# Two blocks of branch gates placed in the softmax pause, and the output projection done tile by tile with four weight buffers

## The reference

```python
def reference(x, positions, w_in, ...):
    proj = einsum('bsd,de->bse', x, w_in)
    aq, ak, av, hq, hf, hi, hg, ga, gh = split(proj)
    attn = sliding_window_gqa_sinks(aq, ak, av, attn_sinks, positions)   # chunks of 64, softmax with a sink
    rec = hgrn2(hq, hf, hi, hg, lb, hgrn_norm_g)                         # chunked recurrence, RMS norm, gate
    mixed = sigmoid(ga) * (attn @ w_proj_attn) + sigmoid(gh) * (rec @ w_proj_hgrn)
    x = layer_norm(ALPHA * x + mixed @ w_out, ln1_g, ln1_b)
    # peer_ffn: 8 heads, top 16 of 128 twice, top 16 of the sums, e = expert numbers, g = softmax of the scores
    hid = einsum('thkd,td->thk', u[e], x); act = gelu(hid)
    ffn = einsum('thk,thkd->td', g * act, v[e])
    return layer_norm(ALPHA * x + ffn, ln2_g, ln2_b)
```

## Time and profile before

| | |
|---|---|
| median of three executions | 1649.82 us (1645.25 to 1654.13) |
| the profiled execution: its own time | 1645.0 us |
| its span in the trace | 1643.2 us |
| PE busy | 1543.6 us, 94% |
| DVE busy | 1131.2 us, 69% |
| DMA over the span | 532.38 MB, 324 GB/s |
| granted PE clock, mean | 0.964 |

### The profile page before, as it was taken

The page is one execution under the profiler, slowest core; times in us unless marked ns, Lnnn a source line. Parts: engine busy times, 40 slices in busy tenths (PEclk is TensorE's granted clock), DMA queues, the critical chain, the costliest instruction groups (busy, mean ns, idle before and its releaser), DMA issues.

```text
span 1643.2 us, 17974 instructions
## 1 busy us (share of the span) xinstructions
PE 1543.6 (94%) x6542; PEld 1098.7 (67%) x6542; DVE 1131.2 (69%) x2364; ACT 270.4 (16%) x543; POOL 610.0 (37%) x518
## 2 busy tenths in 40 slices
PE   8798999789998799999999999889999999999997
PEld 7697778665557566888888888756666544444443
DVE  1413899978769999999979999366556735545523
ACT  2601213621010111111134453100000000000000
POOL 0000543466667463322322223465534633424100
PEclk9898998779999799999999999989999999999999
DMA  7586967777999797998978878999999999999962
GB/s 297 203 275 212 397 228 265 251 246 273 412 398 374 275 403 282 316 330 288 327 255 312 319 277 299 410 383 405 404 408 406 405 402 380 395 393 392 369 218 77
DMA packets 145511, 532.38 MB, mean 324 GB/s; under 512 B 14864, under 2 KB 34064, under 8 KB 133904
## 3 DMA queue, kind: packets, MB, share of 16 engines
q0 software_dynamic: 74016, 269.52, 43.7%
q1 hardware_dynamic: 70256, 244.94, 40.0%
q10 hardware_dynamic: 1152, 16.78, 2.6%
HBM read 503.92 MB, written 27.26 MB: 323 GB/s over the span
## 4 chain that ended last, share of the span: by engine, by line
PE 74%; DVE 12%; DMA 7%; issue 3%; ACT 2%; POOL 0%; SPq 0%; DVEq 0%
PE bank L835 26%; PE bank L860 22%; PE bank L740 7%; PE bank L815 6%; PE bank L853 3%; DMA arena<-v_cols_d 3%; DVE arena L1163 2%; DMA arena<-gates_d 2%; DVE arena L1178 2%; PE bank L775 2%; PE bank L750 2%; PE bank L752 2%; PE bank L587 1%; PE bank L575 1%; DMA arena<-u_cols_d 1%
## 5 line engine op out<-in xcount | busy, mean ns | idle before, releaser
L1592 POOL DMA_INDIRECT arena<-u_d,arena x256 | 319.7, 1249 | 566.4 <-DVE arena L1163 315.9
L860 PE MATMUL bank<-arena 128*128 128x512 f32 x1024 | 448.2, 595 | 16.8 <-DVE arena L1501 14.1
L835 PE MATMUL bank<-arena 128*128 128x256 f32 x2048 | 452.9, 379 | 4.0 <-DMA arena<-u_cols_d 4.0
L835 PEld LDWEIGHTS bank<-arena 128*128 128x128 f32 x2048 | 386.6, 190 | 69.4 <-issue 17.8
L1592 POOL DMA_INDIRECT arena<-v_d,arena x256 | 288.9, 1129 | 362.9 <-DVE arena L1178 287.2
L860 PEld LDWEIGHTS bank<-arena 128*128 128x128 f32 x1024 | 195.1, 191 | 250.7 <-issue 227.2
L1178 DVE SCALAR_TENSOR_TENSOR arena<-arena 128x1024 f32<-128x1024 f32 x256 | 327.9, 1281 | 42.4 <-DMA arena<-v_d,arena 32.2
L1163 DVE CUSTOM_DVE_ANT_0 arena<-arena 128x1024 f32<-128x1024 f32 x256 | 304.2, 1221 | 68.5 <-DMA arena<-u_d,arena 67.9
L1501 DVE TENSOR_TENSOR arena<-arena 128x256 f32<-128x256 f32 x128 | 52.9, 420 | 159.5 <-DMA arena<-act_d 103.1
L1054 ACT ACTIVATE arena<-bank 128x256 f32<-128x256 f32 x128 | 49.2, 384 | 491.2 <-PE bank L835 491.1
L815 PE MATMUL bank<-arena 128*128 128x128 f32 (+1 forms) x512 | 118.9, 394 | 1.4 <-ACT arena L1021 1.4
(11 more groups left out here) (200 smaller groups left out, 1035.6 us busy)
## 6 DMA issues: line engine op xcount, KB each, us to landing
arena<-w_items_d SPq DMA_DIRECT2D x66, 1024.0 KB, 7.2
arena<-u_cols_d SPq DMA_DIRECT2D x128, 512.0 KB, 6.6
arena<-v_cols_d SPq DMA_DIRECT2D x128, 512.0 KB, 8.9
gates_d<-arena ACTq DMA_DIRECT2D x8, 2048.0 KB, 8.2
arena<-gates_d SPq DMA_DIRECT2D x16, 1024.0 KB, 16.7
act_d<-arena SPq DMA_DIRECT2D x8, 1024.0 KB, 9.3
arena<-act_d SPq DMA_DIRECT2D x8, 1024.0 KB, 16.7
arena<-u_d,arena POOLq DMA_INDIRECT x256, 8.7
```

The source lines that it names most:

```text
L835: last = mm(bank[:, 4 + c % 2, 0:ND], u_buf[:, c % UBUFS, k, :], B.act_in[:, k, B.n - ND:B.n], start=k == 0, stop=k == KC - 1)
L860: last = mm(bank[:, 2 * n + half, :], act_slot(i)[:, n * P:(n + 1) * P], v_buf[i % VBUFS][:, half * 512:(half + 1) * 512], start=i == 0, s ...
L1592: pool.indirect_dma_start(rows[:, r % SLOTS, :], None, table, bass.IndirectOffsetOnAxis(eidx[:, t, k:k + 1], 0)).then_inc(landed[r % SLOTS ...
```

## The change

It does five things. (1) `gates(0)` goes ahead of the first `turn_weights`, `gates(1)` behind the first two, in both fronts. They use PSUM banks 0 to 3, wait for all copies of the projections (`proj_out`), and ACT's sigmoids of them (`gate_sigmoids`) stand ahead of the recurrence's output copies; `chunk_kv(0)` waits for these. ACT's last projection copies move ahead of its scaling of the softmax. `turn_rec` now stands directly behind the last `tile_out`. (2) The output projection goes tile by tile, and the first two units sum six of their eight blocks ahead of the wait for the last two. (3) `RING` is 4, and two more items are loaded ahead of x and the input of front B. (4) DVE's rows: none at 161 and 170 within the output projection; `EARLY_ROWS` 196, `PAIR_ROWS` 8, `HOT_ROWS` 18. (5) `SPREAD_END` is 79: the 64 spreads lie in 27 hidden blocks, not in 30.

```diff
--- before.py
+++ after.py
@@ -45,7 +45,7 @@
 RMS_EPS = 1e-6
 
 
-RING, ITEMW = 3, 2048
+RING, ITEMW = 4, 2048
 TW = 256
 N_HQF, N_TOK, N_MIX, N_OUT, N_WQ = 4, TOKW // TW, 3 * KC // 2, D // TW, PH
 TOK_EARLY = 5
@@ -77,18 +77,18 @@
 EXP1_AT = 24
 EXP_AT = 49
 TURN_AT = 51
-SPREAD_AT, SPREAD_END = 52, 82
+SPREAD_AT, SPREAD_END = 52, 79
 ROOT0_Q = 44
 GELU1_AT = FIRST + 12
 PAIR = 2
-EARLY_ROWS, PAIR_ROWS, HALF_ROWS = 204, 7, 8
-HOT_ROWS = 30
+EARLY_ROWS, PAIR_ROWS, HALF_ROWS = 196, 8, 8
+HOT_ROWS = 18
 MID_ROWS = 314
 ACT_BACK_LEAD = 12
 
 
 AT_CUM, AT_SOFT, AT_HGRN, AT_SOFT2, AT_CAUSAL, AT_STATE, AT_REC, AT_MIX, PAIR_STEP = 44, 50, 52, 56, 64, 68, 76, 90, 16
-ODD_STEP, AT_OUT, OUT_STEP, HGRN_STEP, STATE_STEP = 5, 152, 9, 3, 2
+ODD_STEP, AT_OUT, HGRN_STEP, STATE_STEP = 5, 152, 3, 2
 ROUTE_ROWS = 6
 FG_HEAD, ROPE_HEAD = 4, 6
 ROUTE_STEPS = 17
...
@@ -379,8 +379,11 @@
 
         def out_units(F):
 
-            return ([(k, t) for k in range(N_OUT - 2) for t in range(F.nt)]
-                    + [(k, t) for t in range(F.nt) for k in range(N_OUT - 2, N_OUT)])
+            return [(k, t) for t in range(F.nt) for k in range(N_OUT)]
+
+        def gate_bank(m):
+
+            return 2 * m if m < 2 else 4 * (m % 2)
 
         def item(F, k):
 
@@ -463,13 +466,13 @@
                 sp.dma_start(dst, src).then_inc(consts_in, 16)
             for hh in range(2):
                 sp.dma_start(sinkc[CH * hh:CH * hh + CH, :], sinks[hh, :].partition_broadcast(CH)).then_inc(consts_in, 16)
-            for k in range(2, I_MIX):
+            for k in range(2, I_MIX + 2):
                 load(A, k)
             load_x(A)
             load_xT(B)
             for k in range(2):
                 sp.dma_start(ln_gb[:, k, :], ln1[k, :].partition_broadcast(P)).then_inc(ln_in, 16)
-            for k in range(I_MIX, ITEMS):
+            for k in range(I_MIX + 2, ITEMS):
                 load(A, k)
             for k in range(KEPT, ITEMS):
                 load(B, k)
@@ -659,10 +662,28 @@
                                     last = mm(o, before, p, start=False, stop=True)
                     last.then_inc(F.av_done, 1)
 
+                def gates(m):
+                    k = I_MIX + 3 * (m // 2) + m % 2
+                    item_in(pe, F, k)
+                    w = item(F, k).rearrange("p (c n) -> p c n", n=P)
+                    if m >= 2:
+                        pe.wait_ge(F.mix_out, m - 1)
+                    else:
+                        pe.wait_ge(F.proj_out, 2 * N_HQF + N_TOK * nt)
+                    b = gate_bank(m)
+                    for g in range(2):
+                        for c in range(KC):
+                            last = mm(bank[:, b + g, 0:n], w[:, g * KC + c, :], F.act_in[:, c, :],
+                                      start=c == 0, stop=c == KC - 1)
+                    last.then_inc(F.gate_done, 1)
+
+                gates(0)
                 pe.wait_ge(F.reached, V_ZERO)
                 turn_weights(0)
+                turn_weights(1)
+                gates(1)
                 for c in range(F.nc):
-                    if c + 1 < F.nc:
+                    if 0 < c < F.nc - 1:
                         turn_weights(c + 1)
                     times_v(c)
 
@@ -720,26 +741,13 @@
                         last = turn(bank[:, 6 + t % 2, h * P:(h + 1) * P], F.otok[:, t, h, :], ident[:, :])
                     last.then_inc(F.rec_turned, 1)
 
-                pe.wait_ge(F.proj_out, 2 * N_HQF + N_TOK * nt)
+                pe.wait_ge(F.gate_ready, 4)
                 chunk_kv(0)
                 for t in range(nt):
                     chunk_kv(2 * t + 1)
                     tile_out(t)
                     chunk_kv(2 * t + 2)
 
...
                 def branches(m):
                     k = I_MIX + 3 * (m // 2) + 2
@@ -755,9 +763,10 @@
 
                 pe.wait_ge(F.state_ready, states + 1)
                 for m in range(0, KC, 2):
-                    gates(m)
-                    gates(m + 1)
-                    if m == 0:
+                    if m:
+                        gates(m)
+                        gates(m + 1)
+                    else:
                         for t in range(nt):
                             turn_rec(t)
                         pe.wait_ge(F.rec_out, nt)
@@ -765,15 +774,25 @@
                     branches(m + 1)
 
 
+                def sum_out(u, c):
+                    k, t = out_units(F)[u]
+                    w = item(F, I_OUT + k).rearrange("p (c n) -> p c n", c=KC)
+                    return mm(bank[:, u % 4, 0:TW], F.mixT[:, c, t * P:(t + 1) * P], w[:, c, :],
+                              start=c == 0, stop=c == KC - 1)
+
+                pe.wait_ge(F.gate_ready, 2 * KC - 2)
+                pe.wait_ge(F.mix_out, KC - 2)
+                for u in range(2):
+                    item_in(pe, F, I_OUT + u)
+                    for c in range(KC - 2):
+                        sum_out(u, c)
                 pe.wait_ge(F.mix_out, KC)
                 for u, (k, t) in enumerate(out_units(F)):
                     item_in(pe, F, I_OUT + k)
-                    w = item(F, I_OUT + k).rearrange("p (c n) -> p c n", c=KC)
                     if u >= 4:
                         pe.wait_ge(F.y_out, u - 3)
-                    for c in range(KC):
-                        last = mm(bank[:, u % 4, 0:TW], F.mixT[:, c, t * P:(t + 1) * P], w[:, c, :],
-                                  start=c == 0, stop=c == KC - 1)
+                    for c in range(KC - 2 if u < 2 else 0, KC):
+                        last = sum_out(u, c)
                     last.then_inc(F.y_done, 1)
 
 
@@ -970,13 +989,13 @@
                 copy_tok(TOK_EARLY)
                 decays(2)
                 decays(3)
+                for k in range(TOK_EARLY + 1, N_TOK):
+                    copy_tok(k)
                 for c in range(F.nc):
                     act.wait_ge(F.soft_den, c // (F.nc // 2) + 1)
                     for j in range(PAIRS):
                         last = fn(F.SC[:, c, j, :], F.SC[:, c, j, :], ACT.Copy, scale=F.den[:, c, j:j + 1])
                     last.then_inc(F.soft_done, 1)
-                for k in range(TOK_EARLY + 1, N_TOK):
-                    copy_tok(k)
 
                 def copy_wT(c):
                     act.wait_ge(F.w_turned, c + 1)
@@ -995,6 +1014,15 @@
                     fn(F.kendT[:, t, :, :], bank[:, 4 + t % 2, :].rearrange("p (h k) -> p h k", h=HH),
                        ACT.Copy).then_inc(F.kend_out, 1)
 
+                def gate_sigmoids(m):
+                    act.wait_ge(F.gate_done, m + 1)
+                    if m >= 2:
+                        act.wait_ge(F.mix_out, m - 1)
+                    for k in range(2):
+                        fn(F.sig[:, m % 2, k, :], bank[:, gate_bank(m) + k, 0:n], ACT.Sigmoid).then_inc(F.gate_ready, 1)
+
+                gate_sigmoids(0)
+                gate_sigmoids(1)
                 for t in range(nt):
                     act.wait_ge(F.o_done, t + 1)
                     fn(F.otok[:, t, :, :], bank[:, 2 + t % 2, :].rearrange("p (h e) -> p h e", h=HH), ACT.Copy).then_inc(F.o_out, 1)
@@ -1007,11 +1035,8 @@
                             act.wait_ge(F.rec_turned, t + 1)
                             fn(F.recT[:, :, t * P:(t + 1) * P], bank[:, 6 + t % 2, :].rearrange("p (h k) -> p h k", h=HH),
                                ACT.Copy).then_inc(F.rec_out, 1)
-                    act.wait_ge(F.gate_done, m + 1)
                     if m >= 2:
-                        act.wait_ge(F.mix_out, m - 1)
-                    for k in range(2):
-                        fn(F.sig[:, m % 2, k, :], bank[:, 4 * (m % 2) + k, 0:n], ACT.Sigmoid).then_inc(F.gate_ready, 1)
+                        gate_sigmoids(m)
                     if F is B and m == GELU_M:
                         act.wait_ge(hid_ready, 1)
                         fn(hid, hid, ACT.Gelu).then_inc(gelu_done, 1)
@@ -1336,8 +1361,8 @@
                 dve.wait_ge(F.x_in, 16)
                 dve.wait_ge(ln_in, 32)
                 for u, (k, t) in enumerate(out_units(F)):
-                    if t == 0 and k < N_OUT - 1:
-                        rows_until(AT_OUT + OUT_STEP * k)
+                    if u == 0:
+                        rows_until(AT_OUT)
                     dve.wait_ge(F.y_done, u + 1)
                     xs = F.x1[:, t, k * TW:(k + 1) * TW]
                     v.scalar_tensor_tensor(out=xs, in0=xs, scalar=ALPHA, in1=bank[:, u % 4, 0:TW],
```

16 lines of the change are left out of this document (2 added, 14 removed).

## The result

| | before | after |
|---|---|---|
| median, four executions each | 1649.99 us (1645.25 to 1654.13) | 1689.06 us (1679.64 to 1698.43) |
| ratio, 95% interval | | 1.0246 [1.0212, 1.0279] |
| profiled execution, its span | 1645.0, 1643.2 | 1698.4, 1696.5 |
| PE busy, DVE busy | 94%, 69% | 92%, 67% |
| mean granted clock | 0.964 | 0.949 |

The account below looks back on a forecast made before the run. PE was taken to bound the kernel (74% of the span, DVE 12%). 1645.0 + 14.2 at the picks + 3 for clock + 6 for spreads + 4 for the load of gates = 1672 us, range 1650 to 1687.

Parts of the forecast that it names:

- The load of gates: Ahead of combine(0): gathers for 16 more leftover rows may run beside this load, +4 us, range 0 to +8.
- The base: Whole kernel: the terms were added to the profiled execution's own 1645.0 us, 4.8 below the median.
- The spreads: Hidden blocks: ten instead of four carry three spreads, the third waiting for its one-hot tile; +6 us, range 0 to +8.
- Front A: First front: pause not filled, covers lost; gates(2) starts +7 us later (+4.5 to +8.5), partial sums give -1.
- Front B: Second front, at gates(2): pause filled, but lost covers give the gain back; +2 us, range 0 to +4.
- The output projection: Front B, branches' end to third normalised tile: 51.3 to 53.9 us instead of 63.7, taken as -10.5.
- The moved rows: DVE before the picks: 18 more v rows less 4 u rows make the gate weights +19.5 us later.
- the sign: At the picks: PE's list of waits would name one of 12 to 20 us if the forecast held.
- the slow clock behind that wait: PE after its wait at the picks: clock at 1.2 GHz, +3 us, range +2 to +4.
- The table switch: ACT's sigmoids in both fronts: each table load priced at 1.28 us; the skill's 2.66 would add 2.8 in all.

Follow-up runs that it names:

- out_only: Kernel before with four weight buffers, the new load order, partial sums and tile-by-tile output projection, row and spread numbers of before: ratio 0.9992 [0.9970, 1.0015].
- rows_only: Kernel before with only the change's numbers: no rows at 161 and 170, EARLY_ROWS 196, PAIR_ROWS 8, HOT_ROWS 18, SPREAD_END 79: ratio 1.0151 [1.0102, 1.0199].
- spread82: Changed kernel with SPREAD_END back at 82, nothing else: ratio to the kernel before 1.0184 [1.0135, 1.0234].
- hot18_only: Kernel before with HOT_ROWS at 18 instead of 30, nothing else: ratio 1.0078 [1.0052, 1.0103].
- hold8: Kernel before with GpSimd holding the gathers from the ninth row on until front A's query projections are done: ratio 0.9973 [0.9953, 0.9993].

## Why the prediction missed

**The load of gates: the step that failed.** I put "+4, range 0 to +8" for gathers beside the gates load, and it measured +11.4 in the ledger; 12 of the 16 rows alone cost 0.78% [0.52, 1.03]. The mechanism was right, gathers beside that load, and the size was not: I gave the 4 no derivation. The engines were full during that load already, at 396 GB/s; 5.2 MB more of gathers beside it are 13 us at 0.40 MB per us, and its time went from 11.9 to 23.3 us. The 21 us of DMA for the 16 rows, which stood in the same paragraph, would have been too much: only the gathers that run beside the load count, and these were 6.2 MB at most in all profiles. The Trainium skill (DMA: Bandwidth & Descriptors, "Issuing engines are not separate DMA queues") says that transfers of different issuers share the 16 engines, and the trace agrees, with 67.1% and 35.9% for the two queues.

**The base.** 1672 is 1645.0 + 27. The same program took 1659.8 us when it was profiled again, and the difference of the medians applies to 1650. I saw that the profiled execution lay below the median and still added to it. With +27.2 on 1650 it would have been 1677; of the ledger's 38.6 the rest, 11.4, is the load of gates (+7.4), the spreads (+3.7), the fronts and picks (about +2.5), less 2.2 at the end.

**The spreads** measured +9.7 instead of +6. PE's waits ahead of the spreads grew by 7.2 us (9.1 + 3.5 against 5.4), a little more than forecast. Three hidden blocks (48.4/14 = 3.46 us each) move behind the spreads, which alone would change nothing in the sum; the stage became 1.2 us shorter instead of 10.4, so 9.2 were lost in it, and 2.0 of them stand in no wait but in PE's busy time (151.92 us for 930 instructions, against 160.25 for 978). Why is not shown.

**Front A** measured +7.8 for +6 (7 - 1), and at the start of `gates(2)` +9.0 against the second profile (40.1 for 31.1), just outside the +4.5 to +8.5. The waits stand where they were put: 5.54 us for 5.4, 1.89 for 1.2, and 4.34 for 4.2 (the 5.3 with the 1.1 of transposes and copy). The slow clock fell on the 16 gate matmuls (+2.6), which I had only in the upper bound.

**Front B** was right in that the filled pause brings nothing: at `gates(2)` it is +1.0 against the first profile and -1.8 against the second, for the +2 that I took (0 to +4); more than that two profiles can't tell. **The output projection** was right in its size, 53.5 us for 51.3 to 53.9, and misread in its cause: out_only has order, buffers and partial sums, and gains nothing in time. Most of the 10 us come from the rows' absence: 7.9 in rows_only's profile, with the old order.

**The moved rows.** From the third normalisation to the last gate weights DVE needed 871.24 - 568.92 = 302.3 us; it was 277.5 in the first profile and 280.3 in the second of before: +22.0 to +24.8 for 19.5. DVE's waits for v rows that were not there yet (2.56 and 1.80) are in the excess; I had priced the rows as if they were always there. PE's picks came 22.5 us after it was ready, where I had named 12 to 20 as the sign, and the slow clock behind that wait cost 2.3 for 3.

**The table switch.** The 2.66 us of the Trainium skill (ScalarE: Activation LUTs, "What ACT_TABLE_LOAD costs") would have added 2.8 us. The trace of the changed kernel does not agree, like the earlier trace rows: the sigmoids start 0.01 us behind the load of 1.28. Its timeline of ACT:

```profile
74.32 1.28 ACT L1022 ACT_TABLE_LOAD   x1
75.61 0.79 ACT L1022 ACTIVATE arena<-bank 128x128 f32<-128x128 f32 x4
```

## What to carry to other kernels

Where DMA engines are full ahead of a wait, take a moved transfer's bytes over the rate of that stretch as the upper bound of its price (15.7 us for 12 rows, of which 12.8 appeared), and count what will still run beside the load that the wait is for: only that adds to the wait (at most 6.2 MB and 11.4 us here). Then look for an earlier stretch with DMA to spare. Moving transfers out pays only down to the next floor: six and twelve rows fewer, 7.9 and 15.7 us of transfers, took 3.2 and 2.6 us off the wait. Before moving work out of a stage, ask whether the stage's gain and the price behind it are the same work: a reorder and a removal that come together should be tried apart. And make the sum against a median or against two profiles; one stretch of one execution may be a lucky one.

## What the runs showed of the hardware

Two queues share the DMA engines' time. While GpSimd's gathers ran beside SP's loads to the end (the change, spread82, hot18_only), the loads had 35 to 37% of the engines' time and the gathers 66 to 68%, at some 0.40 MB per us in all, and the same load of gates took 23.3 us; with next to no gathers beside it 8.7 and 9.9.

The length of front A's query stretch, 288 matmul instructions of 128 columns (queries and key scores), varies in one and the same program from 35.7 to 50.0 us, and from 35.7 to 51.3 over 17 profiles with unheld gathers, of which only the first was under 41. In the slow phase PE starts an instruction every 0.7 to 2.1 us, while nothing that the profile names holds it, and the granted clock of the whole stretch falls to 0.82, against 0.94 in hold8. The DMA engines are full there, but they are in the short execution too (420 GB/s from 167 to 176 us), so full engines alone don't make the phase. In the three profiles with the gathers held it was 37.1, 36.5 and 35.6 us. That holding gathers shortens it is shown; why PE is slow in it, by its instruction supply or something else, stays open.
